# Two-block transformer on one core: the modulation vectors are summed over partitions by accumulating DMAs instead of TensorE

## The reference

```python
sc, scc = jax.nn.silu(c), jax.nn.silu(c_ctx)
for l in range(DEPTH):                                       # DEPTH = 2
    mod_x = (sc @ w_mod[l] + b_mod[l]).reshape(b_, N_MOD, 1, D_MODEL)    # N_MOD = 9, D_MODEL = 1024
    mod_h = (scc @ w_mod[l] + b_mod[l]).reshape(N_MOD, 1, D_MODEL)
    # sublayers j = 0, 1, 2: vectors 3j (shift), 3j+1 (scale), 3j+2 (gate)
    y = rmsnorm(s, g_pre) * (1 + scale) + shift
    s = s + weight * gate * rmsnorm(f(y), g_post)
```

## Time and profile before

| what | value |
|---|---|
| median of 3 runs | 2373.07 us (2372.89 to 2373.29) |
| span of the profiled execution | 2369.7 us, 29852 instructions |
| median less span | 3.4 us |
| PE busy | 2325.1 us (98%), granted clock 0.998 of full speed |
| DVE busy | 1438.7 us (61%) |
| ACT busy | 1018.8 us (43%) |
| POOL busy | 165.9 us (7%) |
| DMA | 364.38 MB, mean 154 GB/s |

### The profile page before, as it was taken

The page is one execution under the profiler, slowest core; times in us unless marked ns, Lnnn a source line. Parts: engine busy times, 40 slices in busy tenths (PEclk is TensorE's granted clock), DMA queues, the critical chain, the costliest instruction groups (busy, mean ns, idle before and its releaser), DMA issues. The chain is left out here.

```text
span 2369.7 us, 29852 instructions
## 1 busy us (share of the span) xinstructions
PE 2325.1 (98%) x11374; PEld 1910.5 (81%) x11374; DVE 1438.7 (61%) x2174; ACT 1018.8 (43%) x1752; POOL 165.9 (7%) x204
## 2 busy tenths in 40 slices
PE   9999999999999999999999999999999999999998
PEld 7877788777888888877777788887887888767997
DVE  5677765777676733455757674337765345466545
ACT  6554556545632223355545222235222234456444
POOL 1200003000010000022100000001000000411000
PEclk9999999999999999999999999999999999999999
DMA  6556654477555532322114554223676222314654
GB/s 208 198 201 246 225 177 156 157 259 254 175 200 181 184 98 80 107 89 72 54 54 169 204 198 149 89 89 109 221 242 219 80 98 91 123 63 107 205 178 142
DMA packets 120892, 364.38 MB, mean 154 GB/s; under 512 B 13232, under 2 KB 13872, under 8 KB 120752
## 3 DMA queue, kind: packets, MB, share of 16 engines
q1 hardware_dynamic: 118528, 355.63, 44.6%
q0 software_dynamic: 2224, 6.86, 1.1%
HBM read 361.35 MB, written 1.09 MB: 153 GB/s over the span
## 5 line engine op out<-in xcount | busy, mean ns | idle before, releaser
L1826 DVE TENSOR_TENSOR wlo<-raw,whi 128x1024 fp32r<-128x1024 f32 x524 | 645.3, 1235 | 514.1 <-ACT whi L1221 508.9
L1221 ACT CAST whi<-raw 128x1024 fp32r<-128x1024 f32 x524 | 548.3, 1051 | 592.2 <-PE ps L649 577.4
L649 PE MATMUL ps<-xhi,whi 128*128 128x512 f32 (+1 forms) x1280 | 466.3, 364 | 1.4 <-DVE hid L2185 1.4
L649 PE MATMUL ps<-xhi,wlo 128*128 128x512 f32 (+1 forms) x1280 | 464.2, 363 | 0.0
L649 PE MATMUL ps<-xlo,whi 128*128 128x512 f32 (+1 forms) x1280 | 464.2, 363 | 0.0
L649 PE MATMUL ps<-whi,xhi 128*128 128x512 f32 x976 | 396.5, 406 | 10.1 <-ACT xhi L1261 4.5
L649 PE MATMUL ps<-wlo,xhi 128*128 128x512 f32 x976 | 381.9, 391 | 0.0
L649 PE MATMUL ps<-whi,ahi 128*128 128x512 f32 x952 | 373.2, 392 | 3.2 <-DVE wlo L1826 2.3
L649 PE MATMUL ps<-wlo,ahi 128*128 128x512 f32 x952 | 370.6, 389 | 0.0
L649 PE MATMUL ps<-whi,xlo 128*128 128x512 f32 x976 | 287.2, 391 | 0.8 <-DVE xlo L1920 0.8
L649 PEld LDWEIGHTS ps<-xhi,whi 128*128 128x128 f32 x1280 | 241.6, 189 | 45.5 <-issue 5.9
(11 more groups left out here) (176 smaller groups left out, 1654.4 us busy)
## 6 DMA issues: line engine op xcount, KB each, us to landing
raw<-in_w SPq DMA_DIRECT2D x524, 512.0 KB, 3.4
mraw<-in_w_mod SPq DMA_DIRECT2D x144, 512.0 KB, 4.9
grow<-gains POOLq DMA_DIRECT2D x11, 512.0 KB, 6.5
x<-in_x SPq DMA_DIRECT2D x2, 512.0 KB, 5.3
x<-in_ctx SPq DMA_DIRECT2D x1, 1024.0 KB, 7.1
out<-x SPq DMA_DIRECT2D x2, 512.0 KB, 2.6
rmask<-in_rmask SPq DMA_DIRECT2D x1, 768.0 KB, 5.0
ws<-in_ws POOLq DMA_DIRECT2D x2, 256.0 KB, 11.7
```

The lines of the kernel that those rows point to most:

```text
L649: return nc.tensor.matmul(o, lhsT, rhs, start=start, stop=stop, skip_group_check=True)
L1221: nc.scalar.copy(whi[:, slot, :], raw[:, slot, :]).then_inc(hi_done, 1)
L1826: nc.vector.tensor_tensor(wlo[:, slot, :], raw[:, slot, :], whi[:, slot, :].bitcast(F32), ALU.subtract).then_inc(w_split, 1)
```

## The change

Each of the 18 vectors becomes a group of its own: 8 pieces, each both 512-column chunks of a vector, and two accumulators that take turns. PE no longer has any part in it: `mod_sum`, `mod_columns` and their waits go, and so do DVE's copy to `mrow` and the bank it read.

In their place POOL runs `mod_fold` for each vector: seven accumulating DMAs add the upper half of the accumulator's partitions to the lower half (64, 32, 16, 8, 4, 2, 1 partitions, 8 KB a partition for both conditions, 4 KB for one), each waited for before the next is issued; then a store of partition 0 to `msum` in device memory, waited for; then one DMA for each condition that reads `msum` back as a column (1024 elements of 4 bytes) into `mcol`. DVE's `mod_out` waits for `mod_back` and adds the bias. A vector's first piece waits until the vector two before it is stored.

`mod_out` of a vector stands nine units behind its last piece in SUBS 4, 6 and 7 (for the vectors of SUBS 1 and 3, at the start of SUBS 2 and 4). The last four vectors are spread over 24 units with six units each, where they had 16 units with two pieces each. Gates of sublayers 4 and 6 are now both made late; for sublayer 6 POOL's order is: fold of vector 8, `gain_rows(6)`, folds of 9, 10, 11.

```diff
+    for i, each in ((1, [2, 1] * 4 + [2, 2]), (3, [2] * 8)):
         s = SUBS[i]
-    for i, g in ((4, 2), (6, 4), (7, 6)):
+        host([s["u_wide"] + 4 * c + 3 for c, count in enumerate(each, 1) for _ in range(count)])
+    out(0, SUBS[2]["u_wide"] + 8)
+    out(1, SUBS[2]["u_wide"] + 8)
+    out(2, SUBS[4]["u_wide"] + 8)
+    out(3, SUBS[4]["u_wide"] + 8)
+    for i, v in ((4, 4), (6, 8)):
         first = SUBS[i]["u_wide"] + 4
+        host(range(first, first + 32))
+        for k in range(4):
+            out(v + k, first + 8 * k + 16)
+    first = SUBS[7]["u_wide"] + 4
+    host(range(first, first + 16))
+    host([first + 16 + 3 * i // 4 for i in range(32)])
+    out(12, first + 16)
+    out(13, first + 24)
+    for k in range(4):
+        out(14 + k, first + 6 * k + 30)
...
-            def mod_sum(q):
...
-                for i in range(parts):
-                    for j in range(4):
-                        last = mm(ps[32 * j:32 * j + 32, 2 * BANK:3 * BANK], unit_col[:, i, :], accumulator(q)[:, i, j, :],
-                                  i == 0, i == parts - 1)
...
-            def mod_columns(g):
...
-                for nt in range(4):
-                    last = nc.tensor.transpose(bank(3, P * nt, P * nt + P), mrow[:, P * nt:P * nt + P], ident[:, :])
...
                 if s["kind"] == "mix":
                     mixer2(s)
                 tall(s)
+                if i == 1:
+                    act.wait_ge(mod_stored, 16 * 2)
...
                 if k:
-                    dve.wait_ge(mod_added, p - 1)
-                elif q:
-                    dve.wait_ge(mod_summed, q)
+                    dve.wait_ge(mod_added, p)
+                elif v >= 2:
+                    dve.wait_ge(mod_stored, 16 * (v - 1))
...
+            def mod_out(v):
+                l, m = divmod(v, N_MOD)
+                if v == 0:
+                    dve.wait_ge(block2_landed, 16 * n_block2)
+                dve.wait_ge(mod_back, 16 * BACK[v])
+                for i in range(conditions(v)):
+                    last = nc.vector.tensor_tensor(modT[:, l, KD * m:KD * m + KD, i], mcol[:, v % 2, i, :],
+                                                   bmod[:, l, KD * m:KD * m + KD], ALU.add)
                 last.then_inc(mod_taken, 1)
+                if v in LATE_GATES:
+                    dve.wait_ge(mod_taken, v + 1)
+                    gate_columns(SUBS[LATE_GATES[v]]).then_inc(gate_ready, 1)
...
+            def mod_fold(v):
+                there = conditions(v)
+                pool.wait_ge(mod_added, KD * (v + 1))
+                at0 = P // 2
+                while at0:
+                    pool.dma_start(macc[0:at0, v % 2, 0:there, :], macc[at0:2 * at0, v % 2, 0:there, :],
+                                   accum_op=ALU.add).then_inc(mod_folded, 16)
+                    n["folds"] += 1
+                    pool.wait_ge(mod_folded, 16 * n["folds"])
+                    at0 //= 2
+                if v >= 2:
+                    pool.wait_ge(mod_back, 16 * BACK[v - 2])
+                pool.dma_start(msum[v % 2:v % 2 + 1, 0:there, :], macc[0:1, v % 2, 0:there, :]).then_inc(mod_stored, 16)
+                pool.wait_ge(mod_stored, 16 * (v + 1))
+                if v >= 2:
+                    pool.wait_ge(mod_taken, v - 1)
+                for i in range(there):
+                    pool.dma_start(mcol[:, v % 2, i, :], msum[v % 2, i].rearrange("(k p) -> p k", p=P),
+                                   allow_slow_non_contiguous=True).then_inc(mod_back, 16)
...
             for i, s in enumerate(SUBS):
                 nxt = SUBS[i + 1] if i + 1 < len(SUBS) else None
+                if s["i"] == 6:
+                    mod_fold(8)
                 gain_rows(s)
+                for v in {1: (0, 1), 3: (2, 3), 4: (4, 5, 6, 7), 6: (9, 10, 11), 7: range(12, 18)}.get(s["i"], ()):
+                    mod_fold(v)
```

More of the change, by code:

```diff
@@ L153, in mod_plan, with host @@
 def mod_plan():
-    groups, pieces, sum_at, cols_at = [], [], {}, {}
-    def host(g, units, summed, ctx=True):
+    pieces, out_at = [], {}
+    def host(units):
         pieces.extend(units)
[L161 to L167, removed]
-        s = SUBS[i]
-        chunks = [s["u_wide"] + 4 * c + 3 for c in range(1, s["chunks"])]
-        host(g, lead_passes(s, chunks, [2, 1] * 4 + [2, 2]), s["u_wide"] + 41)
@@ L172, in mod_plan, with out @@
-    for i, g in ((4, 2), (6, 4), (7, 6)):
-        first = SUBS[i]["u_wide"] + 4
[L174 to L184, removed]
+    def out(v, u):
+        out_at[u] = out_at.get(u, ()) + (v,)
@@ L185 @@
+    first = SUBS[7]["u_wide"] + 4
[5 more added lines that the diff above has]
+        out(14 + k, first + 6 * k + 30)
+    return pieces, out_at
+PIECE_UNIT, OUT_AT = mod_plan()
 N_PIECES = len(PIECE_UNIT)
-assert sorted(g for g, _ in GROUPS) == list(range(2 * MOD_CHUNKS * DEPTH // KD)) and N_PIECES == 144
+N_VECTORS = N_MOD * DEPTH
+assert N_PIECES == KD * N_VECTORS and sorted(v for vs in OUT_AT.values() for v in vs) == list(range(N_VECTORS))
@@ L188, with conditions @@
 N_P4 = 64
-LATE_GATE = [g for g, _ in GROUPS].index(4)
+LATE_GATES = {2: 4, 8: 6}
+def conditions(v):
+    return 2 if v < N_MOD + 5 else 1
+BACK = [sum(conditions(w) for w in range(v + 1)) for v in range(N_VECTORS)]
 def weight_units():
@@ L336, in build @@
         cT = sb("cT", [P, KD, 2])
[L337 to L338 removed]
+        mcol = sb("mcol", [P, 2, 2, KD])
         modT = sb("modT", [P, DEPTH, N_MOD * KD, 2])
@@ L2209, in tall @@
                             dve.wait_ge(gains_stored, 16 * (n["g"] - 1))
-                        dve.wait_ge(mod_taken, sum(u < nxt["u_wide"] for u in COLS_AT))
+                        there = 2 if nxt["i"] in LATE_GATES.values() else 3
+                        dve.wait_ge(mod_taken, N_MOD * nxt["l"] + 3 * nxt["j"] + there)
                         sub_columns(nxt)
@@ L2631, in _ @@
             dve.sem_inc(gate_done, LEAD4)
-            link(nc.vector.memset(unit_col[:, :, :], 0.0))
-            for i in range(2):
-                nc.vector.memset(unit_col[:, i, i:i + 1], 1.0)
+            link(nc.vector.memset(zero[:, :], 0.0))
             nc.vector.memset(ones[:, :], 1.0)
-            nc.vector.memset(zero[:, :], 0.0)
             link(nc.vector.memset(mhalf[:, :], -0.5))
```

76 lines of the change are left out of this document (17 added, 59 removed).

## The result

The changed kernel takes **2392.9 us** (median of 4 runs, 2391.12 to 2393.61), the kernel before 2372.98 us on the same chip (2371.72 to 2373.29). The ratio is 1.0088, 95% interval [1.0076, 1.01]: **slower by 20 us**. The forecast was 2363, faster by 10. The time lies inside the range (2351 to 2400), on its slower side.

A forecast was written before the change was run, and what follows sets the result against it. PE, busy 98%, was taken as the bound. Work removed, the stall at vector 9 and slower loads gave -20.9 + 8.8 + 2 = -10.1 us against 2369.7; with 3.4 carried over, 2363 us, range 2351 to 2400.

The forecast's parts named there:

- Taken from PE: Sums and transposes removed from PE's program, all on the path: 20.9 us saved.
- C: POOL's chain for each vector, seven folds and the store, up to the read-back: 32.5 us, bounds 8 and 70.
- My sign for the slower case: Folds following each other at over 4.6 us on POOL, with DVE waiting at every `mod_out` in SUBS 7.
- POOL becomes the bound: Rival: POOL's folds outlast the vectors' period, DVE stands still at `mod_out`; 2414 us at 5.5 us a fold; chance 0.25.
- B: Reading `msum` back as columns after the store: 11 us, bounds 4 and 15.
- Vector 9, a loss of 8.8 us: In SUBS 6 fold 9 starts behind the gate's stores, so its column comes late and PE loses 8.8 us.
- the cushion: DVE runs ahead of PE, so a late DVE costs nothing up to about 5 us.
- 5C + B < 181.5: Condition for no loss at the last vectors in SUBS 7, or C < 34.1; taken to hold at 32.5.
- Slower loads in SUBS 1 and 3: 4-byte transfers hold up weight loads at four pairs in SUBS 1 and 3: 2 us in all, bounds 0 and 12.
- reads of 4 bytes: Rival: 18 read-backs cost PE about 1 us each through late weight loads; 2370 to 2379 us; chance 0.1.
- The formula of the Trainium skill: About 2.0 us plus bytes over 436 GB/s for each DMA from POOL: seven folds 16.4 us, C 18.4.
- everything is hidden: Rival: C + B stays below 34.7 us, so vector 9 is in time too; 2352 us, plus 0 to 2; chance 0.2.

The follow-up runs named there:

- E3: Changed kernel without all 126 folds and the sum over partitions; store, 4-byte reads back and waits stay: 2349.93 us, ratio to the kernel before 0.9908.
- E5: Changed kernel plus 28 DMAs, each waited for, behind its last work: accumulating folds and plain copies, 8 and 4 KB a partition; 2494.64 us with this tail.
- E1: Changed kernel with POOL's `gain_rows` of SUBS 6 moved behind folds 8 to 11: 2376.33 us, ratio to the kernel before 1.0018.
- E7: Changed kernel with folds ahead of `gain_rows` in SUBS 4 and 6, and a quarter of the accumulators' memory for each of the last four vectors: 2368.49 us.
- E4: Changed kernel without the folds of vectors 0 to 3 (SUBS 1 and 3) and their sums: 2384.16 us, ratio to the kernel before 1.0047.
- E8: Changed kernel with each fold of 8 partitions or fewer made as two DMAs, one for each condition: 2408.07 us, ratio to the kernel before 1.0143.
- E10: E7's edits and E9's together on the changed kernel: 2358.15 us, ratio to the kernel before 0.9947.
- E9: Changed kernel with four folds instead of seven; eight rows are stored, read back in 32-byte pieces and added by DVE: 2363.49 us, ratio to before 0.9963.
- E2: Changed kernel with the folds as plain copies of the same bytes, without the sum over partitions: 2381.76 us, ratio to the kernel before 1.0038.

## Why the prediction was wrong, point by point

- **Taken from PE, 20.9 us: right.** E3's span is 22.4 us shorter.
- **C, the chain to the read-back, 32.5 us: this step failed.** It measured 39.5 us in the mean, and 41.5 for a vector with two conditions, for which I had priced it: 7.8 for the first fold against 6.5, 6.6 for the second against 5, 24.1 for the five small ones against 17.5, 3.0 for the store against 3.5. The seven folds, 29.0, are what they cost alone (29.1 in E5). The rows they came from, `grow` at 4.0 us at best and 6.5 in the median, were loads of a kernel with hardly any traffic on POOL's queue; I took small folds at below its best, 3.5, as if their price fell with their bytes and the weight loads were not there. They landed after 3.4 to 5.2 us in the median, and the next started 0.3 us behind each landing. My sign for the slower case, over 4.6 us from one small fold to the next, was met (4.8), but the waits that I hung on it, at every `mod_out` of SUBS 7, did not come. The rival "POOL becomes the bound" had its point at C = 35.9, and its sum at C = 39.5 gives (39.5 - 23.7) + (5 x 39.5 - 170.5) - 20.9 = +22, the measured difference of the spans. That is chance: its shares are 16 us in SUBS 6 and 27 in SUBS 7, where 14.0 and 15.3 were lost, and it has none for SUBS 4. (Its sum for 5.5 us a fold has a slip: C + B = 53 is 18 us late at vector 9 by my own 34.7, not 20, so the stalls are 60 and the time 2412.)
- **The first fold behind the gate's rows: missed.** I counted the gate's store and the issue of `grow` as a delay of the start at vector 9, but took 6.5 us for the fold behind it. The 1 MB of `grow` ahead of it in the queue made that 13.2 us in SUBS 6 and 13.6 in SUBS 4, where I had not seen that the same order holds. So the chain of vector 4 was 51.5 us, and DVE waited 9.1 us where I had said that it wouldn't wait.
- **B, the read-back, 11 us: far too much**, 3.9. I had taken the gates' stores as the nearest row, which write 4-byte elements to device memory (landing 9.9 us); reading them is another thing. At vector 9 this error hid most of the two before it, by luck: C + B was 47.7 us against my 43.5, and DVE's wait 17.9 against my 14.
- **Vector 9, a loss of 8.8 us: place and mechanism right, size wrong.** It cost 14.0 us (E1 gets all of it back). The gap was 11.85 us, and nine matmuls at the lower clock add 1.8. That vectors 10 and 11 would be late by nothing was wrong for vector 10: its chain started right behind, took 41.7 us, and DVE waited 6.4 us, hardly more than the cushion.
- **SUBS 7: the deadline that I didn't look at.** I asked when the last `mod_out` would be late, 5C + B < 181.5, and that held (the five chains sum to 171.3, and DVE never waited for a column there). But an accumulator is wanted again after six units: vector 13's fold started at 1739.13 and its store was wanted at 1774.03, 34.9 us later, and landed at 1780.00. At my C of 32.5 this would have held too, by 2 us. The failing step is C, and most of the loss comes from this second, nearer deadline. E7 shows it: 9 us come back with the chain as long as before, and 6.5 stay.
- **Slower loads in SUBS 1 and 3, 2 us: right sign, inside its bounds, too small, wrong cause.** 5.5 to 5.7 us (E3, E4), from the folds, and not from reads of 4 bytes: these were the rival that falls (E3 keeps all of them and loses nothing).
- **The clock was not in the sum at all.** Each of the four gaps was followed by slow matmuls, 8.4 us in all.
- **The cushion, 5 us: right**, 6.1 at vector 9.
- **The formula of the Trainium skill** (DMA: Bandwidth & Descriptors, Anatomy of one DMA — SWDGE (gpsimd) path), from which I had worked out 16.4 us for seven folds: alone on the chip they took 29.1 (E5). It is near for the last fold, 2.0 against a landing of 2.4 us, and for the 8 KB store, 1.8, and low in the middle, where 64 KB accumulating took 4.1 us and copying 2.7. The measurement decides; "everything is hidden" by that way was never near.

What adds up: gaps of 25.7 us on PE, 8.4 at the lower clock and 5.5 in SUBS 1 to 3 are 39.6 of the 43 us between the changed kernel and E3.

One thing more is in the traces: a late chain is a longer one. In SUBS 4 and 6 of all kernels whose folds accumulate one by one (E8 is left out), 38 chains started when DVE's last piece was done, since POOL had waited for it; the second fold, 256 KB, then took 4.8 to 6.5 us to the next start, 5.0 in the median, and seven folds with their store 35.5 in the mean. Another 17 started right behind POOL's last read-back, or less than 1 us later: 6.8 in the median, and 37.8. Nine started behind the gate's rows: 7.4, and 47.4. This goes with the landing of the 256 KB fold, 6.8 us in the changed kernel and 4.8 in E7 and E10: two of these eight chains start early in the changed kernel, all eight in E7 and E10. The losses in SUBS 4 go the same way: against E3 they are 1.5, 1.7, 2.7 and 6.5 us in E4, E1, E5 and the changed kernel, where vector 4's chain is 47.4, 48.6, 49.0 and 51.5 us.

What stays open: what in the start of a chain makes its folds slow (it may be the phase in which they meet loads, but no run held that still), and why the same code gives chains and stages that differ by some us from one trace to the next.

## What to carry to other kernels

A chain of DMAs in which each waits for the landing of the one before is priced more by its count than by its bytes: here a link of 8 KB took 4.3 us in the mean and one of 512 KB 7.8. Each link is dearer beside a stream of loads than alone (38.5 against 29.1 us for seven), and dearer still when the chain starts late; so fold a few times while it halves much, and hand the last eight rows to an engine. When such a chain replaces work that was in order, write down every deadline that hangs on it: the result, the buffer that it sets free, and what stands ahead of its first link in the queue. Here each of the three remedies eased one of them, and together they turn +0.9% into -0.5%.

## What I had not expected of the hardware

- A gap of 3 to 12 us on PE was followed by 8 to 14 matmuls at 0.43 us each instead of 0.23, with a granted clock of 0.5 to 0.6: a gap of 3.06 us cost 5.9.
- 1024 elements of 4 bytes were read from device memory in 3.9 us, and written to it in 9.9, both medians of the changed kernel; 1024 pieces of 32 bytes were read in 4.6 (E9).
- Seven accumulating DMAs from SBUF to SBUF took 29.1 us where seven plain ones took 20.7 (E5): the addition costs 1.2 us a DMA alone, and 0.7 beside the loads (C falls by 5.0 us in E2).
- The first DMA behind 1 MB in POOL's queue took 13.2 and 13.6 us to the next start, with 6.1 where the queue was empty (vectors 9 and 10 in E1).
